# Sums of squares by single-column matmuls ahead of the index scores, and five reorderings

## The reference

```python
proj = jnp.einsum('btd,dn->btn', rmsnorm(h), w_in)          # split into q,k,v,gates,aq,ak,av,iq,ik,iw,...
# gated delta rule (GDN), 8 heads of 128
qkv = silu(causal_conv(concat(q, k, v)))
q = q * rsqrt(sum(q*q, -1) + EPS) * 128**-0.5               # sums of squares per token and head
k = k * rsqrt(sum(k*k, -1) + EPS)
o = chunked_gated_delta_rule(q, k, v, beta, g)              # triangular inverse per chunk, state S
# sparse attention (DSA), 8 heads, 64 of the keys per query
s = einsum(relu(einsum(iq, ik)), iw)                        # index scores
idx = top_k(s, 64); o = softmax(q k_sel) v_sel
merged = sigmoid(ga) * (gdn @ wbg) + sigmoid(gb) * (dsa @ wbd)
h = h + rmsnorm(merged @ w_out);  h = h + rmsnorm(relu(n @ up)**2 @ down)
# second block: retention, gated conv FFN, differential attention, gated conv FFN ("fu1", "fd1")
```

## Time and profile before

| | |
|---|---|
| median of 3 runs | 1268.47 us (1268.13 to 1269.49) |
| the profiled execution, its own time | 1269.95 us |
| its span, first to last instruction | 1268.2 us |
| mean granted TensorE clock | 0.998 |
| busy: PE, PEld, DVE, ACT, POOL | 1254.3, 1169.6, 919.6, 699.2, 154.3 us |

### The profile page before, as it was taken

The page is one execution under the profiler, slowest core; times in us unless marked ns, Lnnn a source line. Parts: engine busy times, 40 slices in busy tenths (PEclk is TensorE's granted clock), DMA queues, the critical chain, the costliest instruction groups (busy, mean ns, idle before and its releaser), DMA issues.

```text
span 1268.2 us, 23324 instructions
## 1 busy us (share of the span) xinstructions
PE 1254.3 (99%) x9041; PEld 1169.6 (92%) x9041; DVE 919.6 (73%) x1290; ACT 699.2 (55%) x1082; POOL 154.3 (12%) x113
## 2 busy tenths in 40 slices
PE   9999999999999999999999999999999999999998
PEld 8997999999989998889998989999889998999986
DVE  6886874878778774447734547999758777999954
ACT  5556465654456343345354546666547567766642
POOL 0000142000000000000000001642200000464310
PEclk9999999999999999999999999999999999999999
DMA  7552332322355555555553444555564444454562
GB/s 300 189 173 101 133 134 101 133 68 68 152 197 188 195 179 185 198 170 182 183 209 109 156 173 167 198 169 195 194 221 171 162 154 163 167 188 175 197 224 93
DMA packets 30315, 212.83 MB, mean 168 GB/s; under 512 B 3488, under 2 KB 3616, under 8 KB 5152
## 3 DMA queue, kind: packets, MB, share of 16 engines
q1 hardware_dynamic: 29088, 206.53, 46.9%
q0 software_dynamic: 1152, 5.24, 1.1%
HBM read 210.71 MB, written 1.05 MB: 167 GB/s over the span
## 4 chain that ended last, share of the span: by engine, by line
PE 86%; DVE 8%; ACT 4%; DMA 1%; issue 1%; SPq 0%; DVEq 0%; ACTq 0%
PE lin L540 50%; PE lin L702 21%; DVE wlo L513 3%; PE lin L2883 2%; PE lin L567 2%; ACT whi L506 2%; PE lin L569 1%; DMA raw<-in_stream 1%; PE aux L2627 1%; PE aux L2599 1%; PE aux L2485 1%; ACT lm L1377 1%; PE aux L725 1%; PE aux L2745 1%; PE aux L2555 1%
## 5 line engine op out<-in xcount | busy, mean ns | idle before, releaser
L513 DVE TENSOR_TENSOR wlo<-raw,whi 128x2048 fp32r<-128x2048 f32 x183 | 427.4, 2338 | 170.8 <-ACT whi L506 170.1
L506 ACT CAST whi<-raw 128x2048 fp32r<-128x2048 f32 x192 | 365.3, 1906 | 179.5 <-DMA raw<-in_stream 147.0
L540 PE MATMUL lin<-xhi,whi 128*128 128x256 f32 (+2 forms) x1616 | 461.5, 286 | 1.0 <-DVE wlo L513 1.0
L540 PE MATMUL lin<-xlo,whi 128*128 128x256 f32 (+2 forms) x1616 | 457.0, 283 | 0.0
L540 PE MATMUL lin<-xhi,wlo 128*128 128x256 f32 (+2 forms) x1616 | 454.7, 281 | 0.0
L540 PEld LDWEIGHTS lin<-xhi,whi 128*128 128x128 f32 x1616 | 304.1, 188 | 3.0 <-DVE wlo L513 1.2
L540 PEld LDWEIGHTS lin<-xhi,wlo 128*128 128x128 f32 x1616 | 306.1, 189 | 0.0
L540 PEld LDWEIGHTS lin<-xlo,whi 128*128 128x128 f32 x1616 | 304.6, 189 | 0.4
L865 POOL TENSOR_TENSOR fu<-fs,ft 128x256 f32<-128x256 f32 x44 | 86.2, 1958 | 259.4 <-ACT fs L1479 259.4
L2292 DVE SCALAR_TENSOR_TENSOR ft<-fy,par,ft 128x254 f32<-128x254 f32 (+1 forms) x176 | 109.5, 661 | 5.9 <-DVE ft L2292 0.2
L540 PE MATMUL lin<-whi,xhi 128*128 128x256 f32 x256 | 74.2, 290 | 0.0
(11 more groups left out here) (454 smaller groups left out, 2123.2 us busy)
## 6 DMA issues: line engine op xcount, KB each, us to landing
raw<-in_stream SPq DMA_DIRECT2D x193, 1024.0 KB, 4.9
gp<-in_gains POOLq DMA_DIRECT2D x6, 512.0 KB, 3.9
c<-in_const SPq DMA_DIRECT2D x1, 1460.0 KB, 16.0
h<-in_x SPq DMA_DIRECT2D x2, 544.0 KB, 4.4
c<-in_const POOLq DMA_DIRECT2D x1, 1024.0 KB, 6.5
ht<-in_xtok POOLq DMA_DIRECT2D x1, 1024.0 KB, 9.6
out<-ht SPq DMA_DIRECT2D x1, 512.0 KB, 2.6
out<-ht SPq DMA_DIRECT2D x2, 256.0 KB, 2.0
```

Source lines behind the costliest of these rows:

```text
L506: nc.scalar.copy(whi[:, s0 % 4], raw[:, s0 % 4]).then_inc(hi_ready, 1)
L513: nc.vector.tensor_tensor(wlo[:, s0 % 4], raw[:, s0 % 4], whi[:, s0 % 4].bitcast(F32), ALU.subtract).then_inc(lo_ready, 1)
L540: ins = nc.tensor.matmul(out, a, b, start=start and n == 0, stop=stop and n == 2)
```

## The change

1. Steps ("l2", 0) and `pe_head_sums` go, with ScalarE's copy and the transposes. Step ("l2t", 0) now makes the sums itself: the squares are the stationary tile, 128 features x 128 (or 16) tokens, and one column of ones moves. That is 24 matmuls for keys (8 heads x 3 chunks of tokens) and 16 for queries (8 x 2), each writing one column. The step stands in front of ("idx", 0, 0), which used to stand in front of ("l2", 0), and the banks turn by one from there on.
2. Around it `load_lo` of slots aq 0 and aq 1 both come after ("av", 0) on VectorE; ak's comes in step ("iq", 0). ScalarE's `load_hi` of aq 1 comes in step "l2t".
3. `load_hi(2, 0)` is issued between the second and the third chunk of the input.
4. In the last layer `second_tile` works in halves of 512 columns instead of pieces of 128 and 256, and SyncE's counts follow.
5. `decayed_queries(2)` is cut in two halves of four heads, at other places of VectorE's order.
6. `branch(0, 0, 2)` is moved from behind the outputs of the first chunk to the place before `masked(1, 6, 1)`.

```diff
@@ -87,10 +87,10 @@
-PROJECT = [("rot", 0), ("iq", 0), ("iq", 1), ("rot", 1), ("rot", 2), ("av", 0), ("idx", 0, 0), ("lo", "aq", 1), ("l2", 0),
-           ("l2t", 0), ("sel", 0), ("idx", 0, 1), ("ak", 0), ("avt", 0), ("top", 0), ("cum", 0), ("idx", 1, 0), ("lo", "aq", 2), ("rot", 3), ("rot", 4),
-           ("aq", 0), ("idx", 1, 1), ("lo", "aq", 3), ("aq", 1), ("rot", 5), ("top", 1), ("aq", 2), ("rot", 6), ("aq", 3),
-           ("rot", 7)]
+PROJECT = [("rot", 0), ("iq", 0), ("iq", 1), ("rot", 1), ("rot", 2), ("av", 0), ("lo", "aq", 0), ("lo", "aq", 1),
+           ("l2t", 0), ("idx", 0, 0), ("sel", 0), ("idx", 0, 1), ("ak", 0), ("avt", 0), ("top", 0), ("cum", 0), ("idx", 1, 0),
+           ("lo", "aq", 2), ("rot", 3), ("rot", 4), ("aq", 0), ("idx", 1, 1), ("lo", "aq", 3), ("aq", 1), ("rot", 5),
+           ("top", 1), ("aq", 2), ("rot", 6), ("aq", 3), ("rot", 7)]
@@ -187,7 +187,6 @@
-        rhead = rstd[0:16]
@@ -400,8 +399,8 @@
             elif step[0] == "avt":
...
-            elif step[0] in ("l2", "l2t", "sel", "cum"):
-                use_next({"l2": "l2sum"}.get(step[0], step[0]))
+            elif step[0] in ("l2t", "sel", "cum"):
+                use_next(step[0])
...
         for t in range(2):
@@ -817,7 +816,7 @@
             for n in range(2):
...
-                sp.wait_ge(S("h_postffn1"), 7 + 2 * n)
+                sp.wait_ge(S("h_postffn1"), 5 + n)
...
             sp.wait_ge(out_done, 48)
@@ -939,6 +938,8 @@
         def act_high_mix(act):
             for c in range(4):
+                if c == 2:
+                    load_hi(2, 0)
@@ -988,7 +989,6 @@
             load_hi(1, 0)
             act_high_mix(act)
-            load_hi(2, 0)
@@ -1081,17 +1081,16 @@
             for step in PROJECT:
...
-                    if step[2] == 0:
-                        load_hi(FIRST[("av", "ak")[step[1]]] + 3, 0)
+                    if step == ("idx", 1, 0):
+                        load_hi(FIRST["ak"] + 3, 0)
+                elif step[0] == "l2t":
+                    load_hi(FIRST["av"] + 3, 0)
                 elif step[0] == "avt":
...
-                elif step[0] == "l2":
-                    b = full(act, "l2sum")
-                    is_free(nc.scalar.copy(rhead[0:16, 0:T1], b[0:16, 0:T1]), "l2sum")
                 elif step[0] in STEP_SLOTS:
@@ -1547,6 +1546,13 @@
             def second_tile(u):
+                if not pre:
+                    own.link(gained(u, 1, 0, 512, 512))
+                    dve.wait_ge(S("root_" + tag), 2)
+                    own.link(nc.vector.reciprocal(rc[:, 1:2], rc[:, 1:2]))
+                    residual(1, 0, 512)
+                    residual(1, 512, D)
+                    return
@@ -1737,8 +1743,8 @@
             for step in PROJECT:
-                if step[0] == "iq":
-                    load_lo(FIRST["iq"] + step[1] + 3, 0)
+                if step == ("iq", 0):
+                    load_lo(FIRST["ak"], 0)
                 elif step[0] == "rot":
@@ -1860,7 +1866,7 @@
-            def triangles(s, g):
+            def triangles(s, g, between=None):
@@ -1868,6 +1874,8 @@
+                if between:
+                    between()
@@ -1940,9 +1948,9 @@
-            def decayed_queries(s):
-                q = qkv[:, 0:8, META + (s - 1) * P:META + s * P]
-                nc.vector.tensor_tensor(q, q, eg[:], ALU.mult).then_inc(S("ke"), 1)
+            def decayed_queries(s, h0, h1):
+                q = qkv[:, h0:h1, META + (s - 1) * P:META + s * P]
+                nc.vector.tensor_tensor(q, q, eg[:, h0:h1], ALU.mult).then_inc(S("ke"), 1)
...
             def right(s, n, g):
@@ -2028,7 +2036,7 @@
-            decayed_queries(1)
+            decayed_queries(1, 0, H1)
@@ -2037,16 +2045,16 @@
             triangles(2, 0)
-            triangles(2, 1)
+            triangles(2, 1, lambda: decayed_queries(2, 0, 4))
             for g in range(2):
...
             compact(2)
             new_state(0)
             blocks(2)
+            decayed_queries(2, 4, H1)
             new_state(1)
-            decayed_queries(2)
-            dve.wait_ge(S("ke"), 2)
+            dve.wait_ge(S("ke"), 3)
@@ -2409,10 +2417,14 @@
             def head_rows():
...
-                after(pe, "l2sum")
                 b = fill("l2t")
-                for c, (t0, m) in enumerate(CHUNKS):
-                    ins = nc.tensor.transpose(b[0:m, 16 * c:16 * c + 16], rhead[0:16, t0:t0 + m], ident[0:16, 0:16])
+                for first, src, squared in ((8, sqk, 1), (0, sqq, 2)):
+                    pe.wait_ge(S("l2sq"), squared)
+                    for c, (t0, m) in enumerate(CHUNKS if first else CHUNKS[:2]):
+                        for n in range(8):
+                            at_n = 16 * c + first + n
+                            ins = nc.tensor.matmul(b[0:m, at_n:at_n + 1], src[:, n, t0:t0 + m], ones[:, 0:1],
+                                                   start=True, stop=True)
...
             def decay_sums():
@@ -2436,8 +2448,6 @@
                 elif step[0] == "idx":
...
-                elif step[0] == "l2":
-                    pe_head_sums(pe)
                 elif step[0] == "l2t":
...
                 elif step[0] == "avt":
@@ -2641,7 +2651,7 @@
             def outputs(s, g):
-                pe.wait_ge(S("ke"), s)
+                pe.wait_ge(S("ke"), 2 * s - 1)
...
                 b = fill(f"o{s}_{g}")
@@ -2688,6 +2698,8 @@
             read_state(1, 1)
+            pe.wait_ge(S("slo"), 2)
+            branch(0, 0, 2)
             masked(1, 6, 1)
@@ -2704,8 +2716,7 @@
             for g in range(2):
                 outputs(1, g)
                 additions(g)
-            pe.wait_ge(S("slo"), 2)
-            branch(0, 0, 3)
+            branch(0, 2, 3)
             pe_spread_blocks(pe, 2)
             read_state(2, 0)
             read_state(2, 1)
@@ -2733,17 +2744,6 @@
-        def pe_head_sums(pe):
...
-            b = fill("l2sum")
-            pe.wait_ge(S("l2sq"), 2)
-            for n in (*range(8, 16), *range(8)):
-                src, t0 = (sqk, 0) if n >= 8 else (sqq, META)
-                a = CCOL["window"] + 15 - n
-                ins = nc.tensor.matmul(b[0:16, t0:T1], c1[:, a:a + 16], src[:, n % 8, t0:T1], start=n == 8, stop=n == 7)
-            is_full(ins, "l2sum")
...
         def pe_token_slot(name, s0, it, j, hi, lo):
...
```

## The result

The changed kernel takes 1270.14 us, the median of 20 runs (1267.72 to 1271.23), beside 1267.98 for the kernel before in the same sessions: a ratio of 1.0015 [1.0008, 1.0021], slower by 0.15%. The forecast of 1265.0 is missed on the side of the rival with the falling clock, which gave 1271.5. The profiled execution took 1270.48, with a span of 1268.4 and a mean granted clock of 0.993, where before had 0.998. All 20 executions of the changed kernel have a mean granted clock between 0.992 and 0.995.

What follows compares the result with a forecast made beforehand. TensorE, busy 1254.3 of 1268.2 us, was taken to bound the kernel. Gains of 1.0 + 0.65 + 1.4 + 0.4 = 3.45 us from the median 1268.47 gave 1265.0; stated range 1263.5 to 1271.0, the forecast's own 1263.8 to 1266.2.

Steps and rivals of the forecast that it cites:

- the rival with the falling clock: Sums: single-column matmuls, mostly loads, let TensorE's clock fall to half; 6.5 us lost against the forecast, 1271.5 us; chance 0.28.
- The start: Slot 2: casting its high part earlier lets VectorE start the low part sooner, removing TensorE's 1.02 us wait; gain 1.0 us.
- The sums at the full clock: Between "av" and "ak": 40 single-column matmuls take 8.0 us, then a 3.2 us chain; "ak" starts 0.65 us earlier.
- The eight small tiles at half price: In the sums: matmuls with 16 stationary columns cost half of full ones, 0.11 us each, 0.9 us in all.
- GDN: 12 moved `branch` matmuls fill TensorE's 1.21 us wait, and halved `decayed_queries` keeps VectorE in time; gain 1.4 us.
- The margin on line 1937: GDN: VectorE's chain ends there 0.14 us before TensorE takes it, the same after both have moved earlier.
- the second rival: A gain is swallowed: GDN's margin fails, or the sums cost 8.9 us and slot 2 lands late; 1266.2 us; chance 0.16.
- The end: Last layer: VectorE's last stretch shrinks from 2.79 to 2.4 us with halves of 512 columns; last DMA leaves 0.4 us earlier.
- The loads overlap: Rival on the sums: they cost far less than their loads, say 2 us, giving 1259.0 us; chance 0.03.

Runs made afterwards that it cites:

- e10_mixed: The changed kernel with 128 moved columns of ones for the 32 full stationary tiles and 64 for the eight small ones, instead of one; 1265.02 us.
- e5_gdn: The kernel before with only the GDN parts (5 and 6: halved `decayed_queries`, moved `branch`); 1266.65 us, ratio 0.9994.
- e1_rest: The kernel before with parts 3 to 6 (start, end and GDN) and the old sums; 1265.34 us, ratio 0.9978.
- e4_in_av: The changed kernel with its 40 single-column matmuls put two or three at a time between the wide matmuls of "av"; 1277.80 us, ratio 1.0070.
- e7_wide64: The changed kernel with 64 moved columns of ones in each matmul of the sums instead of one; 1264.77 us, ratio 0.9977.
- e8_sums_front: Parts 3 to 6 on the kernel before, old sums put ahead of the index scores, VectorE's first weighted sums behind `decay_meta`; 1266.23 us, ratio 0.9983.

## Why the prediction was wrong

The step that failed is the choice in the part on the sums and in its rival: "Against it: TensorE is never idle there, its loads fill the stretch." The sums were priced at the full clock, 8.0 us, as a gain of 0.65, and the fallen clock was given 0.28. They measured a loss: 16.28 - 11.98 = 4.30 us up to "ak" and 1.37 behind it. The clock fell in both profiled kernels that have the new sums in that place with one moved column, and by the mean granted clocks (0.992 to 0.995) in all of their 25 executions. The sentence further up in that rival, that the granted clock "is 1.00 wherever TensorE moves wide operands", was false by the very trace that it spoke of: the windows from 122 to 126 show 0.50 under wide matmuls. Read in time, they would have been a reason to give the rival more than 0.28: the clock could fall here even behind sums that moved 272 columns in each matmul, though no run shows which part of the stretch lets it. The missing 1.48 us between the profiled execution and the median pointed to it too. The stated range, 1263.5 to 1271.0, holds the measured time only because it was stretched for this rival; the forecast's own, 1263.8 to 1266.2, does not.

The rival had the mechanism, and its total of 6.5 us against the forecast (4.2 for the loads, 2.3 for the return) is close in part by luck. In the trace the sums take 12.23 us, 4.2 above 8.0, but not by its working. The fall comes 2.1 us in, not 3.8, so that 5.9 of the 8.0 us were left, and doubled they would have cost 5.9. What the trace has is 44 full records 0.21 us apart instead of 0.11, +4.5, and sixteen small ones for 0.6 us instead of 0.9, -0.3. Behind the sums the rival had 2.3; the trace has 0.7 up to "ak" (3.92 us where 3.2 were forecast) and 1.37 behind its start, 2.1. That is 6.3 in all. The medians show 5.6 (1270.14 against 1267.98 - 3.45), and 0.45 of that is that the other terms and the sums at the full clock brought 3.0 instead of 3.45 (below); against e10_mixed the medians show 5.1 and the profiled executions 5.9. The 20 times of the changed kernel reach from 1267.72 to 1271.23, so that the clock's cost differs between executions; only one was profiled.

The Trainium skill (TensorE: Matmul & The Clock Gate, Part 1: The HAM clock gate) lets the clock follow how busy the engine has been. The trace goes further: an engine that the records show as busy for every microsecond, with weight loads and single columns, falls to 0.50 all the same. The gap of about 25 ns for few columns (the same page, Back-to-back issue gap) is given there for matmuls without their loads, and is not what a matmul with its own load costs here: 0.11 us a record.

Point by point, for the rest:

- *The start*, 1.0 us: right, 1.16. Slot 2 has no wait, and its cast starts at 15.47 and takes 1.90, forecast 15.2 and 1.9.
- *The sums at the full clock*, 0.65 us: right in kind and too large. With the clock held, e10_mixed has 11.61 us from "av" to "ak" against 11.98, a gain of 0.37. The sums take 8.2, not 8.0, and the chain behind them 3.25, not 3.2, with a wait of 0.57 us where 1.4 was to be seen. The eight small tiles at half price, 0.055 us a record, were a guess from the 97 ns of the earlier trace rows, which is how long such a load lasts and not how far two stand apart. It came out with 64 moved columns, where they start 0.057 us apart. With 128 it is 0.11, and in the changed kernel, with one column, 0.03, even at the half clock.
- *GDN*, 1.4 us: right in place, mis-sized. It measured 1.24 in the changed kernel and 1.15 in e5_gdn. The margin on line 1937 held and the second rival did not come; 0.3 went to a longer spread, because part 5 delayed `new_state(1)` and with it a bank that the spread needs. The prediction had looked at VectorE's chain and not at this bank.
- *The end*, 0.4 us: right, 0.45.
- *The loads overlap*: no. Every kernel has 0.11 us a record at the full clock.

The sum of the terms with their measured sizes, 1.16 + 0.37 + 1.24 + 0.45 = 3.2 us, is near what e10_mixed gains over before (1268.02 - 1265.02 = 3.0). So the forecast was that of a kernel whose clock holds, and the changed one lacks for it moved columns, and nothing else that the runs show.

## What to carry to other kernels

Before TensorE's work is replaced by work that is mostly weight loads, look at the granted clock in windows of 1 us around the place, not at its mean: here a dip was already there and went unread. A multiplication can be too small: here more moved columns in the same loads cost next to nothing and bought back 5 us. But that only undid the harm; the way to find out is to run the parts apart, and here the reorderings alone (e1_rest) were as fast. They fill one named gap each, came out within 0.3 us of their working, and could be added up.

## What was not expected of the hardware

- With one moved column the clock fell 2.1 us into a stretch with no idle time and stayed down for 17 us, with 16 it fell 5.6 us in and stayed down for 10, with 64 it fell only behind the stretch, for 3.4, and with 128 not at all. These are one profiled execution each; the mean granted clocks of the others agree, for 1 and 16 columns (none above 0.995) and for 64 and 128 (none below 0.998).
- Wide matmuls between the single columns did not hold it: in e4_in_av three of 272 columns stood before every two or three single ones, and it was at 0.50 from 109.6 to 133.5 us.
- Dips of 3.4 us also follow stretches of short matmuls and waits: in before, e7_wide64 and e8_sums_front. In before such a dip cost 1.55 us, and the times of one kernel lie in two groups about that far apart (e7_wide64: seven runs from 1264.35 to 1264.95, two of 1266.24; e5_gdn: eight from 1266.21 to 1267.26, three from 1268.18 to 1268.41). That the groups are the dips is likely and not shown.
- Records with a full stationary tile start 0.11 us apart with 1, 16, 64 or 128 moved columns at the full clock (0.21 at the half clock, with 1 or 16). With 16 stationary columns they start 0.057 us apart with 64 moved ones and 0.11 with 128, and 0.03 with 1 or 16, at the half clock. The old sums have such tiles with 272 moved columns and take 3.84 us for 16 records, 0.23 or so each. So there the moved columns set the distance, and 128 of them cost as much as one full load, 0.11: up to that many they were free under the full tiles here.
